# A two-block transformer kernel: early modulation on column halves with the norm beside it, late column products moved, causal blocks in falling order

## What is computed

```python
# first block
mx = split(silu(c) @ w_ada + b_ada, 6); mc = split(silu(c_ctx) @ w_ada + b_ada, 6)
hc = modulate(rms_norm(ctx, g_pre_mix), mc[0], mc[1])
hx = modulate(rms_norm(x, g_pre_mix), mx[0], mx[1])
# window attention and a two-way recurrent scan over projections of hx and hc,
# merged with sigmoid gates (project of hx), then
x = x + mx[2] * rms_norm(mix_x, g_post_mix)
x = x + mx[5] * rms_norm(moe_ffn(modulate(rms_norm(x, g_pre_ffn), mx[3], mx[4])), g_post_ffn)
# second block
shift, scale, gate = split(c_2 @ w_ada_2 + b_ada_2, 3)
h = rms_norm(x, norm_w_2) * (1 + scale) + shift
y_a = mla_attention(...) * silu(gate_a)     # 8 heads, causal by chunks of 64
y_b = fox_attention(...) * silu(gate_b)     # 8 heads, causal, with decay
x = x + gate * ((sigmoid(mg_a) * (y_a @ w_branch_a) + sigmoid(mg_b) * (y_b @ w_branch_b)) @ w_out)
```

## Time and profile before

| | |
|---|---|
| Time, median of 3 runs | 3132.25 us (3132.21 to 3143.58) |
| Profiled execution: time, span | 3136.93 us, 3135.1 us |
| PE, DVE, ACT, POOL busy | 83%, 32%, 24%, 11% |
| Opening, until the next weights are called | 84.6 us |
| Gates stage | about 942 to 1069 us |
| Addition stage before the experts | about 1201.6 to 1214.8 us |
| mla and fox stages | 54.4 and 61.0 us |

### The profile page before, as it was taken

The page is one execution under the profiler, slowest core; times in us unless marked ns, Lnnn a source line. Parts: engine busy times, 40 slices in busy tenths (PEclk is TensorE's granted clock), DMA queues, the critical chain, the costliest instruction groups (busy, mean ns, idle before and its releaser), DMA issues. The chain is left out here.

```text
span 3135.1 us, 51899 instructions
## 1 busy us (share of the span) xinstructions
PE 2613.1 (83%) x19294; PEld 1299.5 (41%) x19294; DVE 1013.8 (32%) x2284; ACT 764.4 (24%) x1726; POOL 346.5 (11%) x331
## 2 busy tenths in 40 slices
PE   6788686856789994699988989998999399679998
PEld 1446464645464442333333333333333154355444
DVE  1263636363155424322222222222222502443012
ACT  2133333343060002122222222222222201355000
POOL 0021212130060000000000000000000201244000
PEclk9888798977889997799999999999999599887999
DMA  5100000000307414499999999399968421001112
GB/s 203 57 26 23 6 23 6 23 2 3 108 28 281 147 67 183 184 390 387 387 391 390 387 395 422 150 384 411 402 269 360 148 90 64 19 2 55 54 56 79
DMA packets 114086, 553.36 MB, mean 177 GB/s; under 512 B 12912, under 2 KB 16496, under 8 KB 62352
## 3 DMA queue, kind: packets, MB, share of 16 engines
q1 hardware_dynamic: 97184, 510.27, 40.4%
q10 hardware_dynamic: 10608, 19.91, 1.9%
q0 software_dynamic: 6144, 20.98, 1.8%
HBM read 736.18 MB, written 16.52 MB: 240 GB/s over the span
## 5 line engine op out<-in xcount | busy, mean ns | idle before, releaser
L1353 PE MATMUL moe_gu_ps<-expert_w,xgT 128*64 128x512 f32 x3008 | 667.9, 595 | 39.3 <-PEq L1318 39.2
L1353 PEld LDWEIGHTS moe_gu_ps<-expert_w,xgT 128*64 128x64 f32 x3008 | 252.8, 137 | 445.5 <-issue 445.5
L1379 PE MATMUL moe_down_ps<-expert_w,actT 128*64 128x512 f32 x1504 | 344.6, 597 | 54.8 <-PEq L1318 54.8
L1439 DVE TENSOR_TENSOR biased<-moe_gu_ps,b_gu 128x512 f32<-128x512 f32 x94 | 65.0, 692 | 615.7 <-DVEq L1318 615.7
L1379 PEld LDWEIGHTS moe_down_ps<-expert_w,actT 128*64 128x64 f32 x1504 | 116.7, 136 | 222.2 <-issue 222.2
L1400 ACT ACT_TABLE_LOAD x47 | 60.3, 1283 | 383.0 <-ACTq L1318 383.0
L1868 PE MATMUL ahead_ps<-hT,x 128*128 128x256 f32 (+1 forms) x288 | 128.1, 542 | 5.8 <-PEq L57 5.8
L1280 ACT ACTIVATE xgT<-moe_xg_ps,ffn_shift,ffn_gain 128x64 f32<-128x64 f32 x384 | 119.2, 424 | 41.0 <-PE moe_xg_ps L1274 41.0
L1404 ACT COPY actT<-moe_act_ps 128x256 f32<-128x256 f32 x94 | 35.0, 373 | 375.9 <-ACTq L1318 375.9
L1333 POOL COPY tokens<-token_of 128x1 uint32 x47 | 8.6, 183 | 1040.7 <-POOLq L1318 1040.7
L386 PE MATMUL b2p_ps<-b_w,b_hT 128*128 128x512 f32 (+1 forms) x320 | 119.4, 535 | 1.9 <-PEq L57 1.9
(11 more groups left out here) (690 smaller groups left out, 3721.6 us busy)
## 6 DMA issues: line engine op xcount, KB each, us to landing
expert_w<-in_w_experts SPq DMA_DIRECT2D x576, 1024.0 KB
late_w<-in_w_late SPq DMA_DIRECT2D x12, 2048.0 KB, 8.4
b_w<-in_w_in SPq DMA_DIRECT2D x10, 2048.0 KB, 7.6
ada_w<-in_w_ada SPq DMA_DIRECT2D x6, 2048.0 KB, 12.4
slot_rows<-yb ACTq DMA_DIRECT2D x94, 128.0 KB, 6.2
mix_w<-in_w_in_tok SPq DMA_DIRECT2D x5, 2048.0 KB, 9.9
x<-in_w_rkv SPq DMA_DIRECT2D x5, 1536.0 KB, 7.6
mix_w<-in_w_out SPq DMA_DIRECT2D x2, 2048.0 KB, 7.7
```

Of the source, the lines that this page charges most:

```text
L1353: last = nc.tensor.matmul(ps_gu[SLOTS * j:SLOTS * j + SLOTS, half, :], xgT[:, k, :], w[:, i, at:at + 512], start=(k == 0), stop=(k == KD - 1),
L1379: last = nc.tensor.matmul(ps_dn[SLOTS * j:SLOTS * j + SLOTS, :], actT[:, half, q, SLOTS * a:SLOTS * a + SLOTS], w[:, i, at:at + 512], star ...
L1439: step(nc.vector.tensor_tensor(biased[:, :], ps_gu[:, half, :], b_gu[:, half, :], ALU.add))
```

## The change

It has four parts.

1. `start` and `ada_stage` become one stage, `begin`. The two columns are laid into 64 (`padded`, the rest zero, set by POOL), and the matmuls of even k write rows 0 to 63 of PSUM, those of odd k rows 64 to 127. The copied row block then has 128 partitions, and a matmul with `pick` (two columns, each with a one for both halves) adds the halves and turns them. SP calls the vectors, chunk 0, the identity, chunks 1 to 3, the six tiles of ctx and x, and chunks 4 and 5. ACT's squares and roots stand between the copies of chunks 3 and 4, DVE's scaling between the additions of chunks 2 and 3. What is left of the norm stage is `turn_affine_stage`, with four PSUM buffers instead of two.
2. The late products leave the gates stage for `add_normed_stage` of the first block; the sums get 12 buffers and 7 operations a tile. `finish_modulation` follows the addition, and only the one column that `mix_rows` needs is made before (`mix_row_column`).
3. and 4. `mla` and `fox` hand over their pairs with b falling.

```diff
-                        for k in range(KD):
-                            last = nc.tensor.matmul(ps[0:n_cond, c % 2, :], cond[:, k, :], w_sb[:, c % slots, k, :],
-                                                    start=(k == 0), stop=(k == KD - 1))
+                    for k in range(KD):
+                        at = HALF * (k % 2)
+                        last = nc.tensor.matmul(ps[at:at + HALF, c % 2, :], padded[:, k, :], w_sb[:, c % slots, k, :],
+                                                start=(k < 2), stop=(k >= KD - 2), skip_group_check=True)
...
-                            last = nc.tensor.transpose(ps_c[:, b % 2, m * n_cond:(m + 1) * n_cond],
-                                                       row[:, b % 2, m * P:(m + 1) * P], ident[0:n_cond, 0:n_cond])
+                        last = nc.tensor.matmul(ps_c[:, b % 2, 2 * m:2 * m + 2], row[:, b % 2, m * P:(m + 1) * P],
+                                                pick[:, :], start=True, stop=True, skip_group_check=True)
...
+            sp.dma_start(vec[:, :], d["vectors"]).then_inc(s["vec"], 16)
+            load(0)
+            sp.dma_start(ident[:, :], d["ident"]).then_inc(s["ident"], 16)
+            for c in range(1, slots):
+                load(c)
+            for m in range(n):
+                sp.dma_start(tiles[m], sources[m]).then_inc(s[f"x{m}"], 16)
+            for c in range(slots, n_chunks):
+                sp.wait_ge(s["product"], c - slots + 1)
+                load(c)
...
-    OPS_A_TILE = 6
+    OPS_A_TILE = 7
...
+        self.sum = held.enter_context(self.nc.sbuf_tensor("late_sums", [P, LATE, 512], F32))
...
-        return self.OPS_A_TILE * max(0, t)
+        return min(LATE * KD, self.OPS_A_TILE * max(0, t))
...
-                if q >= 3:
-                    dve.wait_ge(s["late_made"], q - 2)
...
-    def products(self, pe, s, before=None):
-        while self.multiplied < LATE and (before is None or self.sums_by(before - 1) >= KD * (self.multiplied + 1)):
-            q = self.multiplied
-            pe.wait_ge(s["late_sum"], KD * (q + 1))
+    def products(self, pe, s):
+        for q in range(LATE):
...
-                    if late:
-                        late.products(pe, s, before=t)
...
-        finish_modulation(nc, g, late, row_cols)
+        mix_row_column(nc, g, row_cols)
...
-        add_normed_stage(nc, g, "post_mix", [mix[:, m] for m in range(NT_X)], tiles, row[:, :])
+        add_normed_stage(nc, g, "post_mix", [mix[:, m] for m in range(NT_X)], tiles, row[:, :], late=late)
+        finish_modulation(nc, g, late, row_cols)
...
+            if late:
+                @block.tensor
+                def _(pe):
+                    late.products(pe, s)
...
-                      gate=gateT[:, 0, h0 // 2, b * P:(b + 1) * P]) for b in range(NT_X) for h0 in range(0, NH, 2)]
+                      gate=gateT[:, 0, h0 // 2, b * P:(b + 1) * P]) for b in reversed(range(NT_X)) for h0 in range(0, NH, 2)]
...
-                      gate=gateT[:, 1, h0 // 2, b * P:(b + 1) * P]) for b in range(NT_X) for h0 in range(0, NH, 2)]
+                      gate=gateT[:, 1, h0 // 2, b * P:(b + 1) * P]) for b in reversed(range(NT_X)) for h0 in range(0, NH, 2)]
```

More of the change, by code:

```diff
@@ L126, in _, with turn_affine_stage @@
+def turn_affine_stage(nc, name, xn, hT, affine, ident):
+    n = len(xn)
+    with ExitStack() as held:
+        ps = held.enter_context(nc.psum_tensor(f"{name}_ps", [P, 4, 2, 512], F32))
+        with stage(nc, name, "turned", "out_act", "out_dve") as (s, block):
             @block.tensor
             def _(pe):
[L128 to L132, removed]
-                        for k in range(KD):
-                            last = nc.tensor.matmul(ps[0:n_cond, c % 2, :], cond[:, k, :], w_sb[:, c % slots, k, :],
-                                                    start=(k == 0), stop=(k == KD - 1))
[L136 to L142, removed]
-                            last = nc.tensor.transpose(ps_c[:, b % 2, m * n_cond:(m + 1) * n_cond],
-                                                       row[:, b % 2, m * P:(m + 1) * P], ident[0:n_cond, 0:n_cond])
-                        last.then_inc(s["columns"], 1)
@@ L147, in _ @@
+                for m in range(n):
+                    if m >= 4:
+                        pe.wait_ge(s["out_act"], m - 3)
+                        pe.wait_ge(s["out_dve"], m - 3)
+                    for k in range(KD):
+                        last = nc.tensor.transpose(ps[:, m % 4, k // 4, (k % 4) * P:(k % 4 + 1) * P],
+                                                   xn[m][:, k * P:(k + 1) * P], ident)
+                    last.then_inc(s["turned"], 1)
             @block.scalar
             def _(act):
[L149 to L153, removed]
+                for m in range(n):
+                    act.wait_ge(s["turned"], m + 1)
+                    for k in range(4):
+                        gain, shift = affine(m, k)
+                        last = nc.scalar.activation(hT[:, k, m * P:(m + 1) * P], ps[:, m % 4, 0, k * P:(k + 1) * P],
+                                                    ACT.Identity, scale=gain, bias=shift)
+                    last.then_inc(s["out_act"], 1)
@@ L155, in _ @@
             @block.vector
             def _(dve):
[L157 to L162, removed]
+                for m in range(n):
+                    dve.wait_ge(s["turned"], m + 1)
+                    for k in range(4, 8):
+                        gain, shift = affine(m, k)
+                        last = nc.vector.tensor_scalar(hT[:, k, m * P:(m + 1) * P],
+                                                       ps[:, m % 4, 1, (k - 4) * P:(k - 3) * P],
+                                                       gain, shift, ALU.mult, ALU.add)
+                    last.then_inc(s["out_dve"], 1)
@@ L165 @@
+HALF = P // 2
 EARLY = 6
@@ L695, in affine @@
             return gain[:, j, k:k + 1], g.ada[:, k, j:j + 1]
[L697 to L698 removed]
+        turn_affine_stage(nc, "pre", [xn[:, m] for m in range(NT_C + NT_X)], hT, affine, g.ident[:, :])
 def gate_weights(d):
@@ L892, in add_normed_stage, with _ @@
         stat = held.enter_context(nc.sbuf_tensor(f"{name}_stat", [P, 3, n], F32))
-        with stage(nc, name, "squared", "root", "inverse", "scaled", "added") as (s, block):
+        if late:
+            late.ps = held.enter_context(nc.psum_tensor("late_ps", [P, 512], F32))
+        with stage(nc, name, "squared", "root", "inverse", "scaled", "added", "late_made", "late_read") as (s, block):
+            if late:
+                @block.tensor
+                def _(pe):
+                    late.products(pe, s)
             if early is not None:
@@ L908, in _ @@
                                          bias=g.eps_col[:, 0:1]).then_inc(s["root"], 1)
+                if late:
+                    late.keep(act, s)
             @block.vector
```

197 lines of the change are left out of this document (128 added, 69 removed).

## The result

The changed kernel took **3107.53 us** (median of 5 runs, 3097.62 to 3114.64), the kernel before 3135.67 (5 runs) beside it: ratio 0.9907, 95% interval 0.9887 to 0.9926, which is 29 us faster, with an interval of 23 to 35. The forecast was 34.5 less, 3098, with 3083 to 3113 as its range. The profiled execution took 3097.62 us (span 3095.8) against 3136.93 before, 39.3 less. It was the fastest of the five; the ten microseconds between its gain and that of the medians turn out to matter.

A forecast was written before the change was run, and what follows sets the result against it. TensorE bounds the gates and paces the opening's chain (its 83% busy is mostly the untouched experts' loop); it shares the causal ring with GpSimd. -22.1 - 14.5 + 9.5 - 7.4 = -34.5: 3098 against the median 3132.25, range 3083 to 3113.

The forecast's parts named there:

- Opening, -22.1: Opening: half columns make loading set the pace, norm runs beside chunks; next weights called at 62.5 instead of 84.56.
- the earlier trace: Opening's turning: transposes taken at full clock, since 39 in 4.00 us had clock 1.00 in a stage of transposes alone.
- rival A: Whole kernel: clock stays low wherever a stream has gaps, chunk 5 and transposes included; -21, 3111; chance 0.18.
- Gates, -14.5: Gates stage: products leave PE, seven sums a tile; mix_up starts at 1056.2 instead of 1070.66.
- rival D: Gates stage: slower, late loads replace PE as the bound; at 20 us a load 3148; chance 0.03.
- Addition, +9.5: Addition stage: moved products outlast their cover by 8.5 us, and the remaining modulation stage adds 1.0.
- 96 at half clock, 21.3 us: Addition stage: the 96 one-column product instructions never speed up, at 0.222 us each.
- Order, -7.4: Causal stages: falling order gives -1.7 in mla, -8.2 in fox; the gates' matrix stage behind fox loses 2.5.
- wide blocks first keep full clock, the narrow tail loses it: Causal stages: 10 us at half clock put into the narrow tail, so each stage takes 52.7 us.
- C: Opening: the halves don't overlap, chunks stay at 7 us, chunk 5 ends near 55; -27, 3105; chance 0.04.
- B: Addition stage: products reach full clock and are hidden, so 8.5 go; -43, 3089; chance 0.09.
- E: Causal stages: order helps more, both near 48.7 and the next stage fast; -45, 3087; chance 0.10.

The follow-up runs named there:

- e3: Changed kernel with only the opening undone (start, ada_stage and the norm as before): median 3116.6 us, ratio 0.9935 to the kernel before.
- e12: Changed kernel with 128-column late products and the modulation's end folded into the addition stage, but the old opening: median 3103.11 us, ratio 0.9911.
- e1: The changed kernel run again without any edit: median 3109.17 us over 6 runs, ratio 0.9906 to the kernel before.
- e2: Changed kernel with only the falling block order of both causal stages undone: median 3116.8 us, ratio 0.9945 to the kernel before.
- e7: Changed kernel with the 96 late product instructions given 128 moving columns instead of one: one run, 3095.24 us.
- e4: Changed kernel with only the late columns undone (products and six sums a tile back in the gates stage): median 3107.02 us, ratio 0.9905.
- e6: Changed kernel with all eight products of an early chunk on PSUM rows 0 to 63, no halves: one run, 3112.91 us.
- e8: Changed kernel with both causal stages' blocks in the order 1, 3, 2, 0 instead of 3, 2, 1, 0: one run, 3115.35 us.

## Why the prediction was right, and where it was not

**Opening, -22.1: in its stages -21.4, in the program about -8.** The steps hold: 3.65 us a chunk (3.5 forecast), last matmul of chunk 5 at 49.0 (47.9), addition at 50.95 (50.8), weights called at 63.14 (62.5). Chunk 4 was slow as forecast (5.89 against 5.3); chunk 0 was too (5.16), which no term had, but chunk 1's load, landing at 14.56, hid it. The transposes were not at full clock throughout (0.54 from 54 to 57 us, so the earlier trace rows was no sure guide), yet ScalarE set the pace, and its 24 activations took 8.7 us (8.6). The stretch that holds their slow part:

```profile
54.00:57.00 3.00, 3.00 (x17) 3.00 (x16) 2.64 (x8) 2.78 (x8) 0.00 (x0) 0.54 0.01 3
```

Within the turning, TensorE ran only transposes at 0.50 from 53.4 to 56.7 (18 in 3.30 us), and behind them had 1.00 from 56.8 to 59.8 (27 in 3.00 us). The kernel before shows the same: 10.28 us idle, then 16 transposes from 69.45 on, and the clock rises to 1.00 at 72.6. So where the Trainium skill ("TensorE: Matmul & The Clock Gate", Part 4) says that transposes do not bring the full clock, these two traces differ from it, and they are better evidence than the earlier trace rows, where the full clock may be left from the stage before. The section on HAM oscillation of the same page of the Trainium skill, which rival A took to have chunk 5 slow, speaks of waits for DMA that are longer than the matmuls between them. Only chunk 4 had such a wait here (9.13 us), and it was the slow one; chunk 5, without one, took 3.65 us. On that the trace and the section agree.

What failed is the unwritten step behind the opening's sum, that everything after the opening runs as before, only earlier. e3 and e12 show that it does not: about 14 of the 21 us are lost later.

**Gates, -14.5: measured -15.5.** All matmuls ended 110.1 us after the start (111.1), mix_up came 2.6 us later. Taking no gain from the clock over that gap was too careful: mix_up and its followers gave 1 to 3 us. The late loads, rival D, made VectorE wait seven times, 13.5 us in all, and never TensorE.

**Addition, +9.5: measured +6.3, and +8.7 in e1 and e2; with the stages behind it +8 to +13.** The step "96 at half clock, 21.3 us" is 20.61 in e1 and e2; in the first profile the first 22 in 2.5 us ran at 0.96, and all took 18.52. Left out was what comes after: in the four changed profiles the norm and routing stages up to the first expert product ran at a lower clock and took another 1.6 to 4.2 us. e7 shows that both were avoidable. e4 shows that in the whole program gates and addition together gain nothing that the runs can tell, where the forecast had 5.0.

**Order, -7.4: measured -7.8.** That is -2.7 and -7.1 in mla and fox and +2.0 in the gates' matrix stage behind (forecast -1.7, -8.2 and +2.5); e2 against e1 gives 9.7 the same way and 7.6 by the medians. The size was right, in part by luck, since the step "wide blocks first keep full clock, the narrow tail loses it" is wrong in place: half clock came to the wide blocks right behind the fill, and the tail kept full clock but for its last 2.1 us in fox. The gain is that the low stretch in fox is 10 us instead of 31 (2807.9 to 2818.2, against 2837.4 to 2868.1 before), and in mla 7 instead of 14.

**The sum** of the edited stages and those just behind them, taken over e1 and the first profile, is about -36, near the forecast's -34.5, and the measured -29 is less. The forecast's 3098 lay 9.5 us low; 3.4 of these come from the kernel before, whose median was 3132.25 over three runs and 3135.67 over five. That the rest stayed inside the range is partly luck: the range was made for clock losses and hidden products, not for an opening that loses 14 of its 21 us later, which no rival named. By their numbers the rivals C (3105) and A (3111) are nearer to 3107.5 than the forecast, but neither holds: C falls with e6, where chunks without the halves take 7.08 us instead of 3.65, and A's clock losses in the opening and the tails were small. B falls with the seven profiles in which the one-column products took 18.3 us or more, D by the stage's own trace, E in part: mla reached 49 us in e4, e8 and e12, fox never went below 52.4.

## What to carry to other kernels

An edit's gain is not safe until the whole program's median shows it. Undo each part alone, see whether the parts add up to the whole, and where stage times and medians disagree, look for stretches of identical code that changed: the clock of sparse matmul stages, and gaps that move with the number of instructions ahead. A stream of one-column matmuls beside idle time can be cheaper with 128 columns, and in three of five profiles the stages behind it clearly were too.

## What was not expected of the hardware

- TensorE stood still up to 1.9 us, awaiting nothing that the profile shows, at intervals of about 250 matmul and weight-load instructions in the solve stages; 48 instructions more ahead moved the gaps by 45 or 46, and one such stage went from 69.0 to as much as 72.8 us at the same clock (0.92).
- The granted clock rose from 0.50 to 1.00 while TensorE ran nothing but float32 transposes (56.8 us in the changed kernel, 72.6 in the kernel before).
- 96 matmul instructions with one moving column took 20.61 us at 0.50 (18.3 to 20.6 in seven profiles), with 128 columns 13.05 us at 0.83 (11.0 to 13.1 in five).
- The same program's recurrent and window stages took 627 and 639 us in two executions, at 0.83 and 0.80, which is most of a spread of 20 us in the whole.
